# Conditioning rows summed on GpSimd inside the mixer, instead of by products in stages of their own

## What is computed

```
cs  = silu(c)
mod = cs @ w_ada + b_ada                    # w_ada: 1024 x 6144
sh1, sc1, g1, sh2, sc2, g2 = split(mod, 6)
hm = x * (1 + sc1) + sh1
x  = layer_norm(ALPHA * x + (1 + g1) * mamba2_mixer(hm), ln_g[0], ln_b[0])
hm = x * (1 + sc2) + sh2
x  = layer_norm(ALPHA * x + (1 + g2) * moe(hm), ln_g[1], ln_b[1])
```

## Time and profile before

| | us |
|---|---|
| median of 3 runs | 3182.84 (3181.38 to 3186.42) |
| the profiled execution | 3186.32 |
| its span | 3184.6 |
| TensorE busy | 2805.2 (88%) |
| VectorE busy | 2182.5 (69%) |
| GpSimd busy | 1551.1 (49%) |
| ScalarE busy | 1291.1 (41%) |

### The profile page before, as it was taken

The page is one execution under the profiler, slowest core; times in us unless marked ns, Lnnn a source line. Parts: engine busy times, 40 slices in busy tenths (PEclk is TensorE's granted clock), DMA queues, the critical chain, the costliest instruction groups (busy, mean ns, idle before and its releaser), DMA issues. The chain is left out here.

```text
span 3184.6 us, 41434 instructions
## 1 busy us (share of the span) xinstructions
PE 2805.2 (88%) x14781; PEld 2326.7 (73%) x14781; DVE 2182.5 (69%) x2531; ACT 1291.1 (41%) x1598; POOL 1551.1 (49%) x852
## 2 busy tenths in 40 slices
PE   7599999999999999999569999924999999999920
PEld 2288888888888888888527888813888888888810
DVE  2467777687777787777533333353888888888868
ACT  1233333333434333333221111113777677677632
POOL 0023334333334333334201232226999999999965
PEclk9799999999999999999779999966999999999965
DMA  6753545434454435352262223235988769587666
GB/s 236 297 200 129 185 150 189 153 125 175 159 186 172 162 133 189 146 185 93 83 250 94 104 105 118 87 122 199 349 308 296 282 246 355 212 291 272 246 240 241
DMA packets 253612, 618.05 MB, mean 194 GB/s; under 512 B 15911, under 2 KB 98603, under 8 KB 244779
## 3 DMA queue, kind: packets, MB, share of 16 engines
q1 hardware_dynamic: 226250, 520.89, 45.3%
q10 hardware_dynamic: 14688, 53.48, 4.2%
q0 software_dynamic: 12544, 41.97, 3.8%
HBM read 608.64 MB, written 99.93 MB: 222 GB/s over the span
## 5 line engine op out<-in xcount | busy, mean ns | idle before, releaser
L1502 DVE TENSOR_TENSOR piece_lo<-piece_raw,piece_hi 128x2048 fp32r<-128x2048 f32 x187 | 563.8, 3033 | 120.1 <-ACT piece_hi L1602 120.0
L1602 ACT CAST piece_hi<-piece_raw 128x2048 fp32r<-128x2048 f32 x280 | 526.4, 1910 | 238.0 <-DVE ye L1662 157.3
L1502 POOL TENSOR_TENSOR piece_lo<-piece_raw,piece_hi 128x2048 fp32r<-128x2048 f32 x93 | 570.4, 6134 | 21.7 <-ACT piece_hi L1602 19.6
L564 PE MATMUL pj<-hm,w_hi 128*128 128x512 f32 x2048 | 532.4, 405 | 24.1 <-DMA hm<-hm_parts 22.1
L823 DVE SCALAR_TENSOR_TENSOR cv<-ub,par,cv 128x512 f32<-128x512 f32 x384 | 385.2, 1003 | 207.6 <-ACT cv L711 198.6
L564 PEld LDWEIGHTS pj<-hm,w_hi 128*128 128x128 f32 x2048 | 378.4, 190 | 99.8 <-DMA hm<-hm_parts 23.7
L528 POOL TENSOR_TENSOR xw<-xw,t 128x512 f32<-128x512 f32 x64 | 96.8, 1512 | 473.4 <-DVE t L899 473.4
L579 PE MATMUL pz<-wz_hi,hm 128*128 128x256 f32 x2048 | 294.7, 289 | 0.3
L579 PEld LDWEIGHTS pz<-wz_hi,hm 128*128 128x128 f32 x2048 | 264.4, 191 | 6.1 <-DVE wz_lo L801 3.1
L716 ACT ACTIVATE th<-cv 128x512 f32<-128x512 f32 x128 | 81.0, 633 | 436.2 <-DVE cv L823 436.2
L564 PE MATMUL pj<-hm,w_lo 128*128 128x512 f32 x1024 | 254.8, 391 | 0.0
(11 more groups left out here) (279 smaller groups left out, 5936.6 us busy)
## 6 DMA issues: line engine op xcount, KB each, us to landing
hm<-hm_parts SPq DMA_DIRECT2D x32, 4096.0 KB, 13.4
piece_raw<-in_w_gate SPq DMA_DIRECT2D x94, 1024.0 KB
piece_raw<-in_w_up SPq DMA_DIRECT2D x94, 1024.0 KB
piece_raw<-in_w_down SPq DMA_DIRECT2D x92, 1024.0 KB
decay<-acum_rows SPq DMA_DIRECT2D x32, 1024.0 KB, 4.7
w_raw<-in_w_in SPq DMA_DIRECT2D x48, 512.0 KB, 8.2
expert_out<-ye ACTq DMA_DIRECT2D x46, 512.0 KB
hm_parts<-hl SPq DMA_DIRECT2D x4, 4096.0 KB, 16.1
```

Source lines behind the costliest of these rows:

```text
L564: mm = nc.tensor.matmul(pj[m % 2][:], wp[m][:, kk, :], hm[b][:, hp, kk, :], start=q == 0, stop=q == 3 * KK - 1)
L1502: v.tensor_tensor(lo[q][:], raw[q][:], hi[q][:].bitcast(F32), ALU.subtract).then_inc(lo_done[q], 1)
L1602: nc.scalar.copy(hi[q][:], raw[q][:]).then_inc(hi_done[q], 1)
```

## The change

For each turn of the mixer one piece of `w_ada` (128 of the 4096 columns of the four rows, 512 KB) is loaded. GpSimd multiplies it by `cs` and folds its 8 blocks into one by three additions (512, 256 and 128 elements wide in each partition). The result, 128 partitions by 128 columns, is stored into a new table in DRAM, `adad`. In `row_vectors` this table (2 MB) is loaded, and eight products with a matrix of ones sum it over the partitions, for g1, sh2, sc2 and g2. The products of `w_ada` in `row_vectors` and `route` are gone, with their loads. `w_out` has six buffers instead of three, and its low parts are put between the rows. To make room, the tanh is written into `zs`, and the squares into `t1`.

```diff
@@ mixer_steps, SyncE
+            def ada_load(n):
+                if n:
+                    sp.wait_ge(ada_done, n)
+                sp.dma_start(wada[:], w_ada[:, :, 2 * D + n * P:2 * D + (n + 1) * P]).then_inc(ada_in, 16)
+            def ada_store(n):
+                sp.wait_ge(ada_done, n + 1)
+                sp.dma_start(k.adad[:, n * P:(n + 1) * P], asum[:]).then_inc(ada_stored, 16)
@@ before the loop: ada_load(0); in each turn, behind store(i - 1, 0)
+                if i < STEPS:
+                    ada_store(i)
+                if i < LAST:
+                    ada_load(i + 1)
@@ mixer_steps, GpSimd
+            def ada(n):
+                pool.wait_ge(ada_in, 16 * (n + 1))
+                nc.gpsimd.tensor_tensor(wada[:], wada[:], k.cs[:].unsqueeze(2).to_broadcast([P, KK, P]), ALU.mult
+                                        ).then_inc(ada_fold, 1)
+                for q, w in enumerate((KK // 2, KK // 4)):
+                    pool.wait_ge(ada_fold, 3 * n + q + 1)
+                    nc.gpsimd.tensor_tensor(wada[:, 0:w], wada[:, 0:w], wada[:, w:2 * w], ALU.add).then_inc(ada_fold, 1)
+                pool.wait_ge(ada_fold, 3 * n + 3)
+                if n:
+                    pool.wait_ge(ada_stored, 16 * n)
+                nc.gpsimd.tensor_tensor(asum[:], wada[:, 0], wada[:, 1], ALU.add).then_inc(ada_done, 1)
...
+            ada(0)
             for j in range(STEPS):
                 for h in range(2):
                     products(j, h)
+                if j < LAST:
+                    ada(j + 1)
                 for h in range(2):
                     gate(j, h)
@@ ScalarE: squares into t1, tanh into zs
-                    nc.scalar.activation(sq[:, a % 2], xw[:, a], ACT.Square, scale=0.5 * GW ** -0.5,
+                    nc.scalar.activation(t1[h][:, a % 2], xw[:, a], ACT.Square, scale=0.5 * GW ** -0.5,
-                if 2 * i + h:
-                    act.wait_ge(zs_done, 2 * i + h)
-                nc.scalar.activation(zth[:].rearrange("p a n -> p (a n)"), pz[:], ACT.Tanh, scale=0.5
+                if i >= 2:
+                    act.wait_ge(gt, 2 * (i - 2) + h + 1)
+                nc.scalar.activation(zs[i % 2][:, 2 * h:2 * h + 2].rearrange("p a n -> p (a n)"), pz[:], ACT.Tanh,
@@ row_vectors
-        NW = 3
+        NW = 6
-        rows = [k.g1, k.b2, k.a2]
+        rows = [k.g1, k.b2, k.a2, k.g2]
+            sp.dma_start(sums[:], k.adad).then_inc(sums_in, 16)
-                for kk in range(KK):
-                    mm = nc.tensor.matmul(rp[s % 2][:], csb[:, kk, :], wa[s % 2][:, kk, :],
-                                          start=kk == 0, stop=kk == KK - 1)
+                nc.tensor.matmul(rp[s % 2][:], k.ones[:], sums[:, s * 512:(s + 1) * 512], start=True, stop=True
+                                 ).then_inc(row_mm, 1)
@@ row_vectors, VectorE
+            for m in range(4):
+                low(m)
             dve.wait_ge(bias_in, 16 * (len(rows) + 2))
             for s in range(NR):
+                row(s)
+                low(4 + s)
@@ then t = a2 * b1, low(12), b2 += t, a2 *= a1, low(13), a1 and b1 times ALPHA, low(14), low(15)
@@ route, TensorE
-            pe.wait_ge(cs_wide, KK)
-            for n in range(2):
-                pe.wait_ge(wa_in[n], 16)
-                for kk in range(KK):
-                    mm = nc.tensor.matmul(gp[n][:], csb[:, kk, :], wa[n][:, kk, :], start=kk == 0, stop=kk == KK - 1)
-                mm.then_inc(g2_mm, 1)
             pe.wait_ge(slot_ready, 1)
```

More of the change, by code:

```diff
@@ L402, in mixer_steps @@
         y_stored = [sem(f"y_stored{h}") for h in range(2)]
+        ada_in, ada_fold, ada_done, ada_stored = (sem(n) for n in "ada_in ada_fold ada_done ada_stored".split())
         (w_hi_s, w_lo_s, ac_in, zero_set, zero_out, proj, pj_read, halo, tap, th_done, silu, zmm, zth_done, zs_done,
@@ L411, in mixer_steps @@
         w_cols = k.d["w_in"].rearrange("(kk p) n -> p kk n", p=P)
+        w_ada = k.d["w_ada"].rearrange("(kk p) n -> p kk n", p=P)
         LAST = STEPS - 1
@@ L844, in gates @@
                 dve.wait_ge(zth_done, 2 * i + h + 1)
[L845 to L849, removed]
+                z = zs[i % 2][:, 2 * h:2 * h + 2].rearrange("p a n -> p (a n)")
+                nc.vector.scalar_tensor_tensor(out=z, in0=z, scalar=1.0, in1=pz[:], op0=ALU.add, op1=ALU.mult
+                                               ).then_inc(zs_done, 1)
             def segments(i):
@@ L969, in row_vectors @@
         sb, ps, sem = k.makers(ctx)
-        NW = 3
-        wa = [sb(f"wr{b}", [P, KK, 512]) for b in range(2)]
+        NW = 6
         wraw = [sb(f"wo_raw{b}", [P, D]) for b in range(NW)]
-        csb = sb("csb", [P, KK, P])
+        sums = sb("ada_rows", [P, 4 * D])
+        t = sb("row_tmp", [P, D])
         rp = [ps(f"rp{b}", [P, 512]) for b in range(2)]
-        rows = [k.g1, k.b2, k.a2]
+        rows = [k.g1, k.b2, k.a2, k.g2]
         NR = 2 * len(rows)
-        bias_in, cs_wide, row_mm, row_out, chain = (sem(n) for n in "bias_in cs_wide row_mm row_full chain_r".split())
-        wr_in = [sem(f"wr_in{b}") for b in range(2)]
+        bias_in, sums_in, row_mm, row_out, chain = (sem(n) for n in "bias_in sums_in row_mm row_full chain_r".split())
         wo_in = [sem(f"wo_in{b}") for b in range(NW)]
@@ L991, in _ @@
             sp.dma_start(k.b1[:], k.d["ln_b"][0].partition_broadcast(P)).then_inc(bias_in, 16)
[L992 to L997, removed]
         @block.scalar
@@ L1035, in low, with row @@
                                                ).then_inc(lo_done, 1)
[L1037 to L1040, removed]
+            def row(s):
                 dve.wait_ge(row_mm, s + 1)
@@ L1045, in _ @@
                                                in1=half, op0=ALU.add, op1=ALU.add).then_inc(row_out, 1)
+            for m in range(4):
+                low(m)
+            dve.wait_ge(bias_in, 16 * (len(rows) + 2))
+            for s in range(NR):
+                row(s)
+                low(4 + s)
             dve.wait_ge(row_out, NR)
-            t = csb[:].rearrange("p k t -> p (k t)")
-            nc.vector.tensor_tensor(t, k.a2[:], k.b1[:], ALU.mult).then_inc(chain, 1)
+            nc.vector.tensor_tensor(t[:], k.a2[:], k.b1[:], ALU.mult).then_inc(chain, 1)
+            low(12)
             dve.wait_ge(chain, 1)
-            nc.vector.tensor_tensor(k.b2[:], k.b2[:], t, ALU.add).then_inc(chain, 1)
+            nc.vector.tensor_tensor(k.b2[:], k.b2[:], t[:], ALU.add).then_inc(chain, 1)
             nc.vector.tensor_tensor(k.a2[:], k.a2[:], k.a1[:], ALU.mult).then_inc(chain, 1)
+            low(13)
             dve.wait_ge(chain, 3)
-            for row in (k.a1, k.b1):
-                nc.vector.tensor_scalar(row[:], row[:], ALPHA, None, ALU.mult).then_inc(chain, 1)
+            for v in (k.a1, k.b1):
+                nc.vector.tensor_scalar(v[:], v[:], ALPHA, None, ALU.mult).then_inc(chain, 1)
+            low(14)
+            low(15)
             dve.wait_ge(chain, 5)
@@ L1383, in _ @@
             v.tensor_tensor(eq[:], oh1[:], oh2[:], ALU.add).then_inc(slot_ready, 1)
-            dve.wait_ge(g2_in, 16)
-            for n in range(2):
-                dve.wait_ge(g2_mm, n + 1)
-                half = k.g2[:, n * 512:(n + 1) * 512]
-                link(v.scalar_tensor_tensor(out=half, in0=gp[n][:], scalar=1.0, in1=half, op0=ALU.add, op1=ALU.add))
             dve.wait_ge(cnt_mm, 1)
```

32 lines of the change are left out of this document (9 added, 23 removed).

## The result

The changed kernel takes 3221.45 us (median of three, 3215.47 to 3225.7) against 3182.11 for the kernel before on the same chip: ratio 1.0121 [1.0096, 1.0147], slower by 1.2%. A fourth execution took 4904.42 us at a granted clock of 0.552 (the others 0.929 to 0.931) and is left out here; with it the median is 3223.57. The forecast was 3199, slower by 0.5%, in the range 3164 to 3229. Sign and mechanism were right; the price of one term was not.

What follows compares the result with a forecast made beforehand. TensorE was taken to bound the mixer, `w_ada`'s products and their 12 MB the row-vector stage. Mixer +44.5, row stage -28, routing -0.7 sum to +15.8 us: 3199 us from the median 3182.8, slower by 0.5%, range 3164 to 3229.

Steps and rivals of the forecast that it cites:

- That TensorE takes every delay of VectorE in this stage, and where: Mixer: TensorE pauses 0.5, 2.45 or 2.8 us by kind of turn, +44.5 us in all.
- Both waits of the view: Mixer: TensorE idle before `yx` for `st` and before `pz` for `wz_lo`.
- The size of the delay: Mixer: GpSimd and VectorE alternate whole instructions, making VectorE 2.8 us late in an ordinary turn.
- Rival C: Mixer: each turn costs VectorE GpSimd's whole length, 3.6 us late, +70 us, hence 3224 us; chance 0.12.
- A: Mixer: VectorE's room hides the turns everywhere, only -29 is left, 3154 us; chance 0.13.
- B: Mixer: turns cost half, delay 1.4 us, +18 us, hence 3172 us; chance 0.15.
- D: Mixer: a late `ada` load delays GpSimd's `gate`, a few us more; chance 0.02.
- the price of a pause: Mixer: TensorE is at full clock, so each pause is paid in full: 16 x 0.5 + 7 x 2.45 + 7 x 2.8.
- Row stage: Row-vector stage: rows complete 28.5 us after the start, then VectorE 26.3; 54.8 instead of 82.7 us, -28 us.
- Routing: Routing stage: no wait for g2, counting products on a cold TensorE; 3.8 instead of 4.5 us, -0.7 us.
- Ends of the mixer: Mixer's first and last steps: `ada(0)` in a step without scan 0, at worst 1 us; step 31 taken as 0.

Runs made afterwards that it cites:

- a1: Changed kernel without GpSimd's multiply and three additions in the mixer, one-column memset per step instead, loads and stores kept; 3189.31 us, ratio 1.0015.
- a2: Changed kernel with all of GpSimd's arithmetic, but only the first piece loaded and one store; 3257.12 us, ratio 1.0223.
- b1: Changed kernel without GpSimd arithmetic or pieces; three idle VectorE products (about 2.86 us) per turn from the second on instead; 3254.51 us, one run.
- c2: Changed kernel with GpSimd's multiply and additions replaced by memsets about as long, transfers kept; 3191.29 us, one run.
- a3: Changed kernel with GpSimd's work moved behind the roots at the turn's end, waiting for VectorE's last gate; output unchanged; 3157.25 us, ratio 0.9904.
- a4: Changed kernel with the arithmetic left out in the 14 turns around group changes, kept in 17 ordinary turns; 3196.72 us, ratio 1.0035.
- c3: Changed kernel with GpSimd's multiply at its place but without the three additions; 3200.45 us, one run.
- d2: Changed kernel without GpSimd work or pieces; three idle VectorE products (about 3.65 us) in the 16 ordinary turns only; 3209.89 us, one run.
- b2: Changed kernel without GpSimd arithmetic or pieces; four idle VectorE products of 128x1024 (about 4.85 us) per turn instead; 3341.72 us, one run.
- c1: Changed kernel with GpSimd's work moved right behind the turn's roots, without waiting for the last gate; 3283.23 us, ratio 1.031.

## Why the forecast was right in kind and short in size

- **That TensorE takes every delay of VectorE in this stage, and where:** right. Both waits of the view were named, 41.9 us of pauses for 44.5. a1, a2 and b1 show the cause; c2 and a3 show that it is the two engines' turns at SBUF reads. In the first turn of a group over half of the pause falls to `yx`, which the forecast had not named there; the sum is the same.
- **The size of the delay:** right, 2.9 for 2.8 us. Rival C's delay of 3.6 is refuted, although C's 3224 us is the time that was measured: it came by a wrong way. Rivals A (room hides it) and B (half) are refuted by the same rows, D (late load) by the rows that release `yx` and `pz` and by a2, which has the pauses without the loads; a1 adds that the loads cost nothing.
- **The failed step** is the price of a pause. "Every pause that TensorE is given is paid in full" took a pause at its own length; 7 x 2.45 + 7 x 2.8 = 36.8 us for the long ones. In 12 of these 14 turns TensorE then worked at half clock for 3.4 or 6.8 us, and in one more behind a wait for `xw`; TensorE's busy time rose by 28.5 us, 24.6 of it by the clock. a4, c3 and d2 separate it: pauses of 0.4 to 1.7 us, no half clock and only some 0.2 us more than their length; a2, b1, b2 and c1: with pauses of 2.4 us and longer, or two within a few us, it comes in most cases, with no loads (a2), with no GpSimd arithmetic (b1) and at another place (c1). The trace of before held a hint that the forecast passed over: it counted "full clock" in the earlier trace rows as given, while the same table shows 0.50 and 0.79 for the stages in which TensorE waits.
- **Row stage:** right engine, right order; 5.9 us too dear. The transfers came 3.5 us earlier, and the sum of VectorE's durations was taken without their overlap, 2.5 us.
- **Routing:** -0.7 for a measured -0.6 at the named place; another -1.5, 0.65 of it in the wait for `rb`, was not foreseen. **Ends of the mixer:** +3.9 us taken as 0; a1, without arithmetic, has +0.6 ahead of the first unit and +2.2 behind the last, so most of them belong to the rest of the change and not to the arithmetic. Of a1's +4.6 at RS the other 1.8 are in its turns. Which part makes the ends, and the +1.7 of the experts' stage, stays open.

Added up: 44.5 was 41.9 + 28.5, -28 was -33.8, -0.7 was -2.8 with the projection, 0 was 3.9 and 1.7: +39.4 for +15.8.

## What to carry to other kernels

Look for the hole in the engine that shares the port, not only in the one that gets the work: the same four instructions made the kernel 1.2% slower, 3.1% slower or 1.0% faster by place alone. And where TensorE runs without a gap, price a pause by the granted clock behind it. In the 13 traces of this case, from 185 us to the mixer's last unit (pauses of at least 0.3 us; two less than 5 us apart count as a pair):

| TensorE's pause | times | with half clock behind it |
|---|---|---|
| one of 0.3 to 1.73 us | 134 | 0 |
| one of 1.80 and one of 1.84 us | 2 | 2 |
| one of 2.3 to 2.8 us | 64 | 53 |
| one of 3.3 us or more (one of them with 0.4 behind it) | 17 | 17 |
| 1.5 us, then 0.8 to 1.2 us | 21 | 21 |

Without it a pause cost what it lasted and some 0.2 us, with it 1.7 or 3.4 us more. Give spare work out in pieces that stay below the slack of each turn.

## What the hardware showed that was not expected

- Half clock in the midst of a stage in which TensorE is 96.7% busy (94.7% in c1): 13 stretches of 3.4 or 6.8 us after, 30 in c1 (109 us, TensorE idle in 5 of them, so some 52 us lost, 1.6% of the span). The Trainium skill, "TensorE: Matmul & The Clock Gate", section "Part 1: The HAM clock gate (the "warmup" mystery)", puts the ramp's penalty below 1% of a typical kernel's span. The stretches inside the mixer alone come to 27 of 3224 us after (0.8%) and to 1.6% in c1, so that figure doesn't cover a stage with recurring pauses.
- It isn't certain for a given pause: those of 2.42 us at 671.3 and 2.43 us up to 857.69 left the clock full, as did 9 more of about 2.4 us in a2, b1 and b2, while in c1 none did. And in the pairs the second pause isn't always needed: in 7 of the 21 the half clock began before it, 0.6 to 0.9 us behind a pause of 1.5 us, though five lone pauses of 1.51 to 1.73 us elsewhere left the clock full. What decides stays open.
- GpSimd's memsets don't hold up VectorE's two-operand instructions (1.29 us for two), but a copy of 128x3 on VectorE (0.17 us alone), asked for while GpSimd's L538 ran, took 1.78 us in c2, about until the first memset behind it was over.
